# Turns of the identity in five long waits of TensorE, and two reorderings around the small experts, in a two-layer decoder trunk

## The reference

```python
for i in range(DEPTH):
    a = hybrid_mixer(rmsnorm(h, mix_norm_pre[i]), w_in[i], ...)
    h = h + rmsnorm(a, mix_norm_post[i])
    c = memory_cross_attention(rmsnorm(h, xa_norm_pre[i]), rmsnorm(mem, mem_norm[i]), ...)
    h = h + rmsnorm(c, xa_norm_post[i])
    hn = rmsnorm(h, ffn_norm_pre[i])
    f = swiglu(hn, ...) if i % 2 == 0 else moe_swiglu(hn, router_w[j], ...)
    h = h + rmsnorm(f, ffn_norm_post[i])
```

## Time and profile before

| | before |
|---|---|
| time, median of 3 runs (lowest, highest) | 1525.37 us (1525.35, 1525.46) |
| time of the profiled execution | 1524.94 us |
| span of the profiled execution | 1523.0 us |
| mean granted TensorE clock | 0.986 |
| TensorE busy | 1443.7 us, 95% of the span |
| VectorE busy | 1127.5 us, 74% |
| ScalarE busy | 955.0 us, 63% |
| bytes moved, mean rate | 387.36 MB, 254 GB/s |

### The profile page before, as it was taken

One profiled execution on the slowest core, in us unless ns is written; L12 is line 12 of the kernel. 1 busy time (PEld: TensorE's weight loads), 2 busy tenths in 40 slices (PEclk: granted clock), 3 DMA queues, 4 the chain that ended last, 5 costly groups with the idle time before them and its releaser, 6 DMA issues.

```text
span 1523.0 us, 21695 instructions
## 1 busy us (share of the span) xinstructions
PE 1443.7 (95%) x8752; PEld 1265.3 (83%) x8752; DVE 1127.5 (74%) x1085; ACT 955.0 (63%) x1116; POOL 177.1 (12%) x133
## 2 busy tenths in 40 slices
PE   7999998999989999988999999999999999999995
PEld 6979988888879889988999777777777899977774
DVE  4666546666665666456776799999999876789996
ACT  5467446344454575354545598898989544579894
POOL 6100000000015000002000204123040300020400
PEclk9999999999989999997999999999999999999999
DMA  8307524555534065425666799999999866679993
GB/s 348 112 29 304 193 86 149 182 191 193 198 122 164 2 262 181 163 95 213 236 225 249 271 383 422 412 421 416 421 414 422 326 229 249 240 280 413 421 412 126
DMA packets 55137, 387.36 MB, mean 254 GB/s; under 512 B 6368, under 2 KB 6624, under 8 KB 9216
## 3 DMA queue, kind: packets, MB, share of 16 engines
q1 hardware_dynamic: 54112, 384.20, 64.7%
q10 hardware_dynamic: 432, 1.08, 0.2%
q0 software_dynamic: 496, 0.74, 0.1%
HBM read 383.90 MB, written 2.10 MB: 253 GB/s over the span
## 4 chain that ended last, share of the span: by engine, by line
PE 64%; DVE 26%; issue 5%; ACT 5%; DMA 0%; ACTq 0%; SPq 0%; DVEq 0%
DVE w_low L1289 15%; PE banks L1790 10%; PE banks L1791 10%; PE banks L1792 10%; PE banks L2112 7%; PE banks L1958 5%; PE banks L2114 5%; DVE low_more L1289 5%; PE banks L1788 3%; PE banks L1789 3%; PE banks L1960 3%; ACT w_high L844 1%; PE banks L2007 1%; DVE after_heads L1572 1%; PE banks L1993 1%
## 5 line engine op out<-in xcount | busy, mean ns | idle before, releaser
L1289 DVE TENSOR_TENSOR w_low<-raw,w_high 128x2048 fp32r<-128x2048 f32 x258 | 588.1, 2296 | 170.0 <-ACT w_high L844 169.9
L844 ACT ACTIVATE w_high<-raw 128x2048 fp32r<-128x2048 f32 x258 | 492.2, 1920 | 161.8 <-PE banks L1960 65.8
L1788 PE MATMUL banks<-w_high,rows 128*128 128x512 f32 (+1 forms) x424 | 161.6, 387 | 3.0 <-ACT after_heads L1113 2.5
L1789 PE MATMUL banks<-w_low,rows 128*128 128x512 f32 (+1 forms) x424 | 156.8, 375 | 0.0
L2112 PE MATMUL banks<-rows,w_high 128*128 128x320 f32 x544 | 142.8, 308 | 2.1 <-DVE rows L1284 1.3
L2114 PE MATMUL banks<-rows,w_low 128*128 128x256 f32 x544 | 142.2, 278 | 0.0
L1790 PE MATMUL banks<-rows,w_high 128*128 128x256 f32 x480 | 138.5, 288 | 3.9 <-DVE rows L1290 3.9
L1791 PE MATMUL banks<-rows,w_high 128*128 128x256 f32 x480 | 137.8, 287 | 0.0
L1792 PE MATMUL banks<-rows,w_low 128*128 128x256 f32 x480 | 137.6, 287 | 0.0
L1790 PE MATMUL banks<-w_high,rows 128*128 128x256 f32 x480 | 137.5, 286 | 0.0
L1792 PE MATMUL banks<-w_high,rows 128*128 128x256 f32 x480 | 135.8, 283 | 0.0
(11 more groups left out here) (235 smaller groups left out, 3229.0 us busy)
## 6 DMA issues: line engine op xcount, KB each, us to landing
raw<-in_pieces_dram SPq DMA_DIRECT2D x291, 1024.0 KB, 7.0
raw_more<-in_pieces_dram SPq DMA_DIRECT2D x66, 1024.0 KB, 8.1
phase<-in_mem_dram SPq DMA_DIRECT2D x2, 1024.0 KB, 7.1
early<-in_constants_dram SPq DMA_DIRECT2D x1, 1088.0 KB, 14.1
h_res<-in_x_dram SPq DMA_DIRECT2D x2, 512.0 KB, 4.1
phase<-in_mix_norm_post_dram SPq DMA_DIRECT2D x2, 512.0 KB, 4.8
phase<-in_xa_norm_post_dram SPq DMA_DIRECT2D x2, 512.0 KB, 6.9
kept<-h_res SPq DMA_DIRECT2D x2, 512.0 KB, 3.1
```

What stands on the lines that cost most here:

```text
L844: return act.activation(out_, in_, ACT.Copy, scale=scale)
L1289: return dve.tensor_tensor(out_, in_, plain(high), ALU.subtract)
L1788: pe.matmul(dst, stay[0], move[0], start=start, stop=False, skip_group_check=True)
L1789: return pe.matmul(dst, stay[0], move[1], start=False, stop=stop, skip_group_check=True)
```

## The change

Three edits. First, TensorE gets `keep_busy(dst, times)`, which turns the identity `times` times into a bank that the next stage writes anew: 12 times at the start, 16 behind mixT of layer 0, 26 behind xo in both layers, 42 behind the dense SwiGLU and 14 behind the logits, 136 in all. Second, at the end of an expert of at most 128 tokens ScalarE splits the piece ahead before it moves the two output halves, and no longer behind them. Third, in step 0 of such an expert VectorE multiplies ahead of the last two shares and no longer behind them (for steps with two pieces of up; the first lines of the diff are only constants).

```diff
+AT_START, BEHIND_TURN, BEHIND_XO, BEHIND_DENSE, BEHIND_LOGITS = 12, 16, 26, 42, 14
 ...
                 wait_mixed(act, piece(e, "down", WIDE_STEPS - 1))
+                ahead(piece(e, "down", WIDE_STEPS - 1))
                 first_half, second_half = halves_of_output(y_sb, blocks)
                 move(*first_half).then_inc(y_first, 1)
                 move(*second_half).then_inc(y_second, 1)
-                ahead(piece(e, "down", WIDE_STEPS - 1))
 ...
                     ahead(piece(e, "up", s, of_step(s) - 1))
+                    if two:
+                        multiply(s)
                     if e and s == 0:
                         add_share(e - 1, 2)
                         add_share(e - 1, 3)
                     if two:
-                        multiply(s)
                         for i in range(2 if s else 0):
                             ahead(piece(e, "down", s - 1, i))
 ...
+            def keep_busy(dst, times):
+
+                for _ in range(times):
+                    pe.transpose(dst[:, 0:P], ident, ident)
 ...
             pe.nop().then_inc(tile_full, 1)
+            keep_busy(banks[:, 0, :], AT_START)
             for layer in range(DEPTH):
                 turn_stage(layer, "mixT", xn, xn_ready, TT * (3 * layer + 1))
+                if layer == 0:
+                    keep_busy(bank(tile(layer, "u")), BEHIND_TURN)
 ...
                 pieces(layer, "xo", mix_parts)
+                keep_busy(bank(tile(layer, "ffT")), BEHIND_XO)
                 turn_stage(layer, "ffT", xn, xn_ready, TT * (3 * layer + 3))
 ...
                     pe.nop().then_inc(hidden_turned, STEPS)
+                    keep_busy(banks[:, 4, :], BEHIND_DENSE)
 ...
                 ins.then_inc(logits_full, 1)
+                keep_busy(banks[:, 5, :], BEHIND_LOGITS)
```

## The result

| | before | changed |
|---|---|---|
| median (lowest, highest) of the executions side by side | 1525.41 us (1524.44, 1526.85) | 1515.96 us (1514.52, 1516.95) |
| ratio, with its 95% interval | | 0.9937 (0.9925 to 0.9949) |
| profiled execution | 1524.94 us | 1515.45 us |
| its span, mean granted clock | 1523.0 us, 0.986 | 1513.6 us, 0.992 |

The change takes about 9.6 us (8 to 11) off. Forecast were 1513.0 us, a range of 1510 to 1518 and a gain of 12.2: the direction and the range held, the gain was 2.6 smaller than the sum. The time lies outside the range of the likeliest case (1511.5 to 1514.5) and close to the first rival's 1516.5. One slow execution of the changed kernel took 3649.93 us and one of e3 2859.19; both are left out of ranges and ratios, and with them the medians would be 1516.24 and 1524.53.

A forecast was written before the change was run, and what follows sets the result against it. TensorE was taken to set the pace through most of the program, another engine in the small experts. Terms of 2.3, 0.4, 1.9, 3.0 and 4.6 summed to 12.2 us, giving 1513 us, range 1510 to 1518.

The forecast's parts named there:

- the likeliest case: Whole kernel: all terms come within some tenths, 1511.5 to 1514.5 us; chance 0.42.
- the first rival: Clock lost again in what is left of the waits; mixT gives 0.6, router 1.0: 1516.5 us; chance 0.2.
- The start and ffT of layer 0: Turns at the start let u run at full clock, 2.3 us; ffT's tiles come earlier, 0.4 us.
- The bound of a loss: Start: with all 44 turns at half clock they end at 15.9 against 14.75, a loss of 1.1 us.
- the rival that rested on it: Turns of the identity don't count for the clock; only the experts gain: 1522.8 us; chance 0.05.
- mixT and u of layer 1: 42 turns fill the wait; 0.4 at the tiles, then u at full clock: 1.9 us, bounds 0.4 and 2.2.
- the clock is lost again in what is left of the waits: Idle time behind the 42 turns and gaps between halves of xn drop the clock: 1516.5 us; chance 0.2.
- ffT and router of layer 1: Logits at full clock take 3.5 us, VectorE no longer waits for them: 3.0 us, bounds 1.0 and 4.2.
- The small experts: Earlier split and multiply give 1.15 us at each of four entries, 4.6 us; bounds 0 and 1.3 each.
- The cover of the halves: Small experts: output halves, ready at 941.9, stay hidden by 0.6 us ahead of the share; otherwise at most 1.8 lost.
- the rival of a DMA bound: DMA becomes the bound of the small experts, 3.2 us instead of 4.6; 1514.5 to 1515.5 us; chance 0.13.

The follow-up runs named there:

- e3: The kernel before with only ScalarE's split moved ahead of the two output halves, no turns: 1524.46 us, ratio 0.9998.
- e9: The changed kernel once more, nothing edited, for a second profiled execution: 1515.28 us, ratio 0.9933 to before.
- e2: The kernel before with the five groups of turns alone, without the two reorderings: 1520.05 us, ratio 0.9963.
- e10: The kernel before once more, nothing edited: 1527.86 us in its one execution.
- e11: e5 without the 14 turns behind the logits: 1512.77 us, ratio 0.9921 to before.
- e5: The changed kernel with 32 turns behind xo, 58 behind the dense SwiGLU, 3 between the halves of xn, 10 behind mixT of layer 1: 1512.28 us, 0.9916 to before.
- e8: The changed kernel with the extra turns of e5 and e7 together, and 5 and 8 turns at the end of each layer's heads: 1514.21 us, 0.9926 to before.
- e7: The changed kernel with 3 turns behind each four of the logits' products, 12 behind the logits and 9 behind the rank matmuls: 1515.07 us, 0.9938 to before.
- e6: The changed kernel without the 42 turns behind the dense SwiGLU: 1514.37 us, ratio 0.9928 to before.
- e4: The kernel before with only VectorE's multiply moved ahead of the last two shares, no turns: 1521.53 us, ratio 0.9979.
- e1: The kernel before with the two reorderings at the small experts alone, no turns: 1520.98 us, ratio 0.9977.
- e12: The kernel before with only the 12 and 16 turns of the start and both reorderings: 1518.66 us, ratio 0.9956.

## Why the prediction was right, and where its sizes were off

**The start and ffT of layer 0: right.** 2.60 and 2.64 us in the two profiles of the changed kernel, 2.7 forecast. u takes 20.72 - 14.77 = 5.95 us (6.0 forecast). The bound of a loss, all turns at half clock, was never near: the 16 turns behind mixT take 1.91 us. That turns raise the clock by themselves is shown by these rows, since TensorE had done nothing else up to then. The Trainium skill (TensorE: Matmul & The Clock Gate, Part 4: PE-mode transpose) says that full clock does not engage in that mode; for the f32 transposes here the trace disagrees, and the rival that rested on it fell.

**mixT and u of layer 1: this is the term that failed.** The sum had 1.9; the profiles show 0.06 and 0.25, below its lower bound of 0.4. The step that failed is that the clock, held up by the turns, would still be up when u runs. It was up until 445.0 (444.0 in e9), then fell during mixT's turns, behind the gaps that the turns of the identity leave (2.02 us ahead of the first half, and in the first profile 0.33 between the halves). With the drop so late, in the first profile u's first 4.9 us were low (3.8 before), and it took 7.97 us and not 7.52: u lost nearly what mixT had won. This is the rival "the clock is lost again in what is left of the waits" (1516.5), right in this half of it. The row that spoke against it, a stretch half idle at a clock of 1.00 (102.30 to 105.70 in the earlier trace rows), was one execution: e2, e10 and e11 have a low stretch at or just behind that place. e5, e8 and e11 leave gaps of 0.3 us at most ahead of the halves, and in all three the clock is 1.00 throughout and the stretch takes 9.73 us, 2.1 less than before. By the measure of the table above the step is 2.28 us in all three: the term was there to be had, somewhat larger than forecast. With the turns of the changed kernel it was different in each execution: 0.06, 0.25, 0.42 (e7) and 1.42 us (e2). e6 has no 42 turns and 1.38: its clock fell early in the idle wait and was back in time for u. So what decides is whether the drop is over when u starts, and the 42 turns alone do not see to that.

**ffT and router of layer 1: 2.84 us at expert 0, and 1.34 in e9; forecast 3.0.** At the gather it is 2.4 and 2.2; in e9 the gather then ran at half clock. The steps in detail: VectorE's wait for the logits went from 2.54 to 0.31 us, as said. But the logits took 5.05 and 4.92 us, not 3.5. The clock falls while they run in every profile in which it was at 1.00 when they began (in e11 only 0.1 us before their end), also with TensorE busy all the time (e7), so its level behind ffT was not the whole matter. The 14 turns were costed as hidden even at half clock (3.0 us against a wait that would have grown to some 3); in fact they ended 0.9 us behind the chosen experts. e11 without them shows 2.97 us of plain waiting and a rank on time. Whether they pay at all is not settled: the changed kernel's first profile had the clock back for the gather, e9's did not, and e5 with them is 0.5 us faster than e11 without them by the medians, on different chips and within their intervals.

**The heads of layer 1: not in the sum.** The drop at 537 cost 0.96 us in the first profile and is absent in e9 and all other profiles, in which the way from f to ffT takes 225.8 to 225.9 us. The same program runs with it and without it, so the edits alone do not bring it.

**The small experts: right, a little better.** 5.16 us, and 5.30 in e9, against 4.6: 1.3 at each of four entries, at the upper bound. The 1.15 was costed for both reorderings together; e4 gives that with the multiply alone, and the split adds 0.15 to it. Of the 0.85 us of VectorE's wait 0.35 were to be kept; 0.85 - 0.48 = 0.37 were, and e3 shows 0.3 an entry. The cover of the halves held: shares show no wait but the one at the end of the program, 1.4 us, that was there before. DMA moves 421 GB/s in the window where it moved 418, with the same share of 1.01, so the rival of a DMA bound fell.

**The sum.** Forecast and first profile, term by term: 2.7 and 2.60; 1.9 and 0.06; 0 and -0.96; 3.0 and 2.6 (2.84 at expert 0, of which 0.27 goes again by the end of expert 1); 4.6 and 5.16. That is 12.2 against 9.4, and nearly all of the difference is mixT and the heads. The rival that comes out nearest, 1516.5, had mixT right in the main but the router at 1.0, and knew nothing of the heads: that it hits the time is in part chance.

**What stays open.** Why the clock falls within the logits with TensorE busy, and what decides where it falls in an execution, no run here tells. In every profile in which it fell there, TensorE had waited 0.7 to 0.8 us just ahead of the logits, and no run fills that gap, so the logits themselves are not shown to be the cause. The experts' term is the same in all executions (5.2 to 5.3 in the profiles of changed, e1, e9, e11 and e12). But e1's median gained only 3.5 us with an interval of 1.4 to 5.6, so by the times alone its size stays loose.

## What to carry to other kernels

Fill a wait up to the work behind it: here the turns that left 2 us free still had u start at the low clock in three of four profiles, and those that left 0.3 us gave the full 2.1 us in three of three. A fill behind work that ends at a low clock is to be sized at half clock: the 14 turns here ended 0.9 us too late. Where two engines pass work to each other in turn, put the instruction that the other waits for ahead of those that nobody needs yet; such a gain of 1.3 us an entry comes back the same in every execution, while one that rests on the clock has to be read from several profiles.

## What the runs showed of the hardware that was not expected

- The same program meets the clock's drops at different places in different executions: before has 0 or 3.4 us low at about 104, and 3.4 or 10.2 us at about 248; with e9, twelve executions of before went from 1520.03 us (mean clock 0.990) to 1527.85 us (0.983). From expert 0 to the end of the experts, at full clock, two executions of before agree to 0.05 us in 788.
- 32 matmuls of 8 columns, issued without a gap, did not keep the clock: it went from 1.00 to half in the midst of them in the changed kernel, e2, e6 and e9 (2.1 to 2.8 us behind their start) and in e5 (0.9 us), and with turns of 128 columns between them in e7 (2.3 us). In e11 it held for 3.6 of their 3.71 us. A gap of 0.77 us stood ahead of them each time.
- The level returned during transposes alone (the start), during matmuls of u, and behind an idle wait once transposes had begun (e6, at 446.6).
